# Feed-forward outputs of the first block: the upper four feature blocks of two weight tiles stand ahead of the wait for the SwiGLU products

## The reference

```python
def swiglu(h, w_in, w_out):
    a, g = jnp.split(h @ w_in, 2, axis=-1)
    return (jax.nn.silu(a) * g) @ w_out

    # in first_block, layer i
    x_lat = x_lat + mod_l[5] * swiglu(modulate(x_lat, mod_l[3], mod_l[4]), ffn_w_in[i], ffn_w_out[i])
    if need_ctx:
        x_ctx = x_ctx + mod_c[5] * swiglu(modulate(x_ctx, mod_c[3], mod_c[4]), ffn_w_in[i], ffn_w_out[i])
```

## Time and profile before

| | |
|---|---|
| median of 3 runs | 3102.27 us |
| lowest, highest | 3101.55, 3102.42 us |
| span of the profiled execution | 3102.3 us |
| TensorE busy | 2967.6 us, 96% |
| VectorE busy | 1898.2 us, 61% |
| ScalarE busy | 1184.0 us, 38% |
| mean rate of the DMAs | 153 GB/s |

### The profile page before, as it was taken

One profiled execution on the slowest core, in us unless ns is written; L12 is line 12 of the kernel. 1 busy time (PEld: TensorE's weight loads), 2 busy tenths in 40 slices (PEclk: granted clock), 3 DMA queues, 4 the chain that ended last, 5 costly groups with the idle time before them and its releaser, 6 DMA issues.

```text
span 3102.3 us, 49288 instructions
## 1 busy us (share of the span) xinstructions
PE 2967.6 (96%) x20168; PEld 2652.2 (85%) x20168; DVE 1898.2 (61%) x2575; ACT 1184.0 (38%) x1300; POOL 23.4 (1%) x33
## 2 busy tenths in 40 slices
PE   8999999999989899899999898999999999999998
PEld 5896887887867689899889887998899898888996
DVE  5754666675566655455557667654555476676554
ACT  5212223221154454333343534443433344425444
POOL 0000000000000000010000000000000000000000
PEclk9999999999999999999999999999999999999999
DMA  7420343444421145454544324555445543234454
GB/s 284 170 101 16 140 158 127 166 169 149 163 87 65 45 151 189 163 189 177 202 172 178 112 83 150 182 184 190 179 177 189 203 163 136 97 136 161 178 190 149
DMA packets 72066, 474.42 MB, mean 153 GB/s; under 512 B 8017, under 2 KB 9201, under 8 KB 20337
## 3 DMA queue, kind: packets, MB, share of 16 engines
q1 hardware_dynamic: 58352, 418.47, 37.1%
q10 hardware_dynamic: 11520, 41.95, 4.1%
q0 software_dynamic: 2048, 11.92, 1.0%
HBM read 471.26 MB, written 1.05 MB: 152 GB/s over the span
## 4 chain that ended last, share of the span: by engine, by line
PE 86%; DVE 7%; ACT 3%; DVEq 2%; issue 1%; DMA 0%; ACTq 0%; SPq 0%
PE ps L405 21%; PE ps L406 20%; PE ps L407 20%; PE ps L411 6%; PE ps L413 5%; PE ps L412 5%; DVE w_lo L1730 2%; PE ps L682 1%; ACT w_hi L1233 1%; DVE w_lo L1784 1%; PE ps L649 1%; PE ps L769 1%; PE ps L788 0%; PE ps L1125 0%; DMA raw<-in_ws 0%
## 5 line engine op out<-in xcount | busy, mean ns | idle before, releaser
L1730 DVE TENSOR_TENSOR w_lo<-raw,w_hi 128x2048 fp32r<-128x2048 f32 x371 | 850.6, 2293 | 685.8 <-ACT w_hi L1233 684.6
L1233 ACT CAST w_hi<-raw 128x2048 fp32r<-128x2048 f32 x369 | 702.3, 1903 | 1267.2 <-PE ps L407 910.4
L405 PE MATMUL ps<-l_hi,w_hi 128*128 128x256 f32 x2896 | 833.7, 288 | 16.2 <-DVE l_lo L1871 4.6
L406 PE MATMUL ps<-l_lo,w_hi 128*128 128x256 f32 x2896 | 824.0, 285 | 0.0
L407 PE MATMUL ps<-l_hi,w_lo 128*128 128x256 f32 x2896 | 823.7, 284 | 0.0
L405 PEld LDWEIGHTS ps<-l_hi,w_hi 128*128 128x128 f32 x2896 | 560.5, 194 | 28.0 <-issue 19.9
L406 PEld LDWEIGHTS ps<-l_lo,w_hi 128*128 128x128 f32 x2896 | 560.8, 194 | 0.3
L407 PEld LDWEIGHTS ps<-l_hi,w_lo 128*128 128x128 f32 x2896 | 560.4, 193 | 0.0
L405 PE MATMUL ps<-h_hi,w_hi 128*128 128x512 f32 (+1 forms) x1088 | 388.1, 357 | 20.1 <-DVE h_lo L1791 15.5
L406 PE MATMUL ps<-h_lo,w_hi 128*128 128x512 f32 (+1 forms) x1088 | 382.9, 352 | 0.0
L407 PE MATMUL ps<-h_hi,w_lo 128*128 128x512 f32 (+1 forms) x1088 | 382.8, 352 | 0.0
(11 more groups left out here) (453 smaller groups left out, 4003.1 us busy)
## 6 DMA issues: line engine op xcount, KB each, us to landing
raw<-in_ws SPq DMA_DIRECT2D x396, 1024.0 KB, 4.8
aT<-in_aw ACTq DMA_DIRECT2D x80, 512.0 KB, 3.6
ln_rows<-in_lnrow POOLq DMA_DIRECT2D x4, 1024.0 KB, 6.1
X<-in_xt SPq DMA_DIRECT2D x1, 2048.0 KB, 17.2
dist<-in_ret_dist POOLq DMA_DIRECT2D x1, 2048.0 KB, 14.0
relB<-in_relb POOLq DMA_DIRECT2D x2, 768.0 KB, 5.8
c_rows<-in_crow POOLq DMA_DIRECT2D x1, 1024.0 KB, 8.4
out<-X SPq DMA_DIRECT2D x1, 1024.0 KB, 4.8
```

The lines of the kernel that those rows point to most:

```text
L405: mm(out_, w_hi[:, s % SPLIT, blk], rhs_hi, start=start, stop=False)
L406: mm(out_, w_hi[:, s % SPLIT, blk], rhs_lo, start=False, stop=False)
L1233: nc.scalar.copy(w_hi[:, s % SPLIT], raw[:, raw_slot(s)]).then_inc(hi_done, 1)
L1730: tt(w_lo[:, raw_slot(s)], raw[:, raw_slot(s)], w_hi[:, s % SPLIT].bitcast(F32), ALU.subtract).then_inc(lo_done, 1)
```

## The change

TensorE's `ffn_out` takes the number of the `operand_ready` it needs as an argument, and waits for it later. It first waits for all groups but the last two, and multiplies tile 0 and then tile 1 for the upper four output blocks alone (m = 4 to 7, banks 4 to 7). Then it waits for all groups and multiplies both tiles for the lower four (banks 0 to 3), and raises `tile_used` for each behind its lower half. Only then does it wait for `operand_ready`, and tiles 2 to 9 follow in two turns of four. Tile 10 is as before. Tiles 0 and 1 read hidden blocks 0 to 3. No matmul is added or removed, and the other engines' programs are the same. The change is in both feed-forward parts.

```diff
-            def ffn_out(phase, cols, number, after=None):
+            def ffn_out(phase, cols, ready, after=None):
 
                 width = cols.stop - cols.start
+                s0 = PH[phase][0]
+
+                def part(t, blocks):
+                    for ci in range(2):
+                        for m in blocks:
+                            ins = product(ps[:, m, 0:width], ci * DC + m, s0 + t, hid_hi[:, 2 * t + ci, cols],
+                                          hid_lo[:, 2 * t + ci, cols], t == 0 and ci == 0, False)
+                    return ins
+                pe.wait_ge(sums_taken, group(phase, 0, 0))
+                for t in range(2):
+                    wait_tile(s0 + t, 0)
+                    part(t, range(4, DC))
                 pe.wait_ge(sums_taken, group(phase, 0, 2))
-
-                def body(first):
-                    def run(i, u, s, turn):
-                        wait_tile(s, turn)
-                        for ci in range(2):
-                            blk = bass.ds(i * 8 + 2 * (u + first) + ci, 1)
-                            for m in range(DC):
-                                ins = product(ps[:, m, 0:width], ci * DC + m, s, hid_hi[:, blk, cols], hid_lo[:, blk, cols],
-                                              first == 0 and ci == 0, False)
-                        ins.then_inc(tile_used, 1)
-                    return run
+                for t in range(2):
+                    part(t, range(4)).then_inc(tile_used, 1)
+                pe.wait_ge(operand_ready, ready)
+
+                def body(i, u, s, turn):
+                    wait_tile(s, turn)
+                    for ci in range(2):
+                        blk = bass.ds(i * 8 + 2 * (u + 2) + ci, 1)
+                        for m in range(DC):
+                            ins = product(ps[:, m, 0:width], ci * DC + m, s, hid_hi[:, blk, cols], hid_lo[:, blk, cols],
+                                          False, False)
+                    ins.then_inc(tile_used, 1)
...
-                tiles(phase, 0, pe, body(0), 0, 1)
-                tiles(phase, 0, pe, body(1), 1, 8)
-                tiles(phase, 0, pe, body(9), 9, 1)
+                tiles(phase, 0, pe, body, 2, 8)
                 tiles(phase, 0, pe, last, 10, 1)
...
-            pe.wait_ge(operand_ready, 4)
-            ffn_out("ffn_out0", slice(0, TT), 0, lambda c: squares(2, slice(0, TT), [c], SQ, 0))
+            ffn_out("ffn_out0", slice(0, TT), 4, lambda c: squares(2, slice(0, TT), [c], SQ, 0))
...
-            pe.wait_ge(operand_ready, 8)
-            ffn_out("ffn_out1", slice(0, T), 1)
+            ffn_out("ffn_out1", slice(0, T), 8)
```

## The result

| | before | changed |
|---|---|---|
| median | 3102.27 us | 3089.53 us |
| lowest, highest of 5 runs each | 3101.55, 3103.85 us | 3089.37, 3090.45 us |
| span of the profiled execution | 3102.3 us | 3087.3 us |

The ratio is 0.9957, with a 95% interval of 0.9946 to 0.9968: 12.7 us faster, by the interval between 9.9 and 16.8 us. The forecast was 3088.0 us in a range of 3086.0 to 3092.0 us.

What follows compares the result with a forecast made beforehand. TensorE was taken to bound the kernel (86% of the chain), losing time in idle and cold start ahead of both ffn_out phases. Gains of 10.27 and 3.97 us made 14.2 us: 3088.0 us, in a range of 3086.0 to 3092.0.

Steps and rivals of the forecast that it cites:

- The clock as a second price: At both ffn_out waits: besides the idle, TensorE restarts at 1.2 GHz, costing 2.45 us in ffn_out0 or 1.53 in ffn_out1.
- ffn_out0, 10.27 us: First feed-forward: tile 1 ends at 755.29 instead of 765.56; 7.8 us of idle and 2.45 of cold start go.
- margin at tile 2: ffn_out0: half a tile of matmuls, 5.44 us, covers tile 2's preparation of about 4.6 us, leaving 0.8 us, no stall.
- releaser of tile 3's high part: ffn_out0: tile 3's high part begins only behind the aT loads, which wait for VectorE to free buffers, at T0 + 9.87.
- ffn_out1, 3.97 us: Second feed-forward: tile 2 ends at 1263.03 instead of 1267.00, despite two new idles of about 1.5 us each.
- No clock lost behind the new idles: ffn_out1: nothing was taken for clock loss behind the two short idles; a cold start each, 1.53 us, was the upper bound.
- Rows 10 and 12: Profile rows of before: idles of 2.23 and 2.37 us behind full work, followed by stretches at clock 1.00.
- The sum, 14.2 us: Whole kernel: 10.27 us from ffn_out0 plus 3.97 us from ffn_out1, giving 3088.0 us.
- Nothing needs scaling: Whole kernel: the profiled span of 3102.3 us was taken as equal to the median of the runs, 3102.27 us.
- The clock in ffn_out1: Rival: the clock swings back behind the short idles, one or two cold starts, 1.5 to 3.1 us; chance 0.12.
- a broken margin: Rival: tile 1's or 2's margin in ffn_out0 fails, or later phases lose the gain, some 1 to 3 us; chance 0.10.
- The ring of aT loads: Rival: ffn_out0's chain of weight parts, ada halves and aT loads, 9.6 us a tile, eats the gain from 13.0; chance 0.03.

Runs made afterwards that it cites:

- run that kept the clock: Kernel before with 32 extra matmuls of 512 columns in the wait ahead of ffn_out0, their result overwritten: 3101.96 us against 3103.39.
- Six blocks ahead: Changed kernel, but in ffn_out0 six output blocks instead of four stand ahead for each of tiles 0 and 1: 3093.47 us.
- last bank late: Changed kernel, but in ffn_out1 tile 0 for seven output blocks, tile 1 for block 7, tile 0's last block, then tile 1's rest: 3087.11 us.
- form with one tile: Changed kernel, but in ffn_out1 only tile 0 is split, and tile 1 follows whole: 3090.37 us.
- ffn_out0 alone: Changed kernel with the old order put back in ffn_out1, so the new order stands in ffn_out0 only: 3093.72 us.
- 16 matmuls: Changed kernel with 16 extra matmuls of 512 columns between ffn_in0 and ffn_out0, their result overwritten: 3092.78 us.

## Why the prediction was right, point by point

- **The clock as a second price.** Right in kind; 2.45 us at ffn_out0 was the longest of four values (1.5 to 2.45), so the term is some 0.6 us above their mean of 1.8. The sizes come from stretches; the run that kept the clock couldn't show the price in the time. Taking it from one profiled execution was the weak step.
- **ffn_out0, 10.27 us.** Measured in the trace: 10.27. The margin at tile 2 was 0.88 us (0.8 said), the releaser of tile 3's high part changed to the aT buffers as said, 9.7 us behind the high part of tile 2 (759.26 - 749.54; about 9.6 said). Six blocks ahead showed the same cover from its other side.
- **ffn_out1, 3.97 us.** Measured: 3.86, with idles of 1.50 and 1.63 us (about 1.5 said, both on the low part of a tile). The run with the last bank late shows that short covers are their whole cause: too little of tile 0 ahead of tile 1 for the first, tile 0 held too long for the second.
- **No clock lost behind the new idles.** Right here, at 1.00 behind both, but with luck, for the reasons given don't carry. Rows 10 and 12 were read as idles of 2.23 and 2.37 us that full work makes harmless. At the place of the first of them the changed kernel has an idle of 2.25 us (first product at 1863.11), with the same matmuls and a clock of 1.00 in the 10.7 us ahead of it, and the clock behind it was 0.58 for 2 us. That the work between the two new idles protects the second was not tested. That it was close is shown as well by the form with one tile, where 2.69 us of idle cost 1.4 us. The Trainium skill ("TensorE: Matmul & The Clock Gate", "Why this matters for your kernels") warns only of gaps longer than that one; the trace differs, and the measurement decides.
- **The sum, 14.2 us.** The medians moved by 12.7, inside the interval of the ratio, and the spans of the two profiles by 15.0. Of these 15.0, 14.13 lie at the two sites (10.27 + 3.86); the rest is what other stages gained and lost: 2.1 us less elsewhere in the first block and 1.2 us more in the second. That the site stretches come out to 0.1 us says that the mechanism is right; it says nothing of the size of the cold start, since the stretch of before is the one the forecast was read from. Of the 1.5 us between 14.2 and 12.7 the cold start would explain 0.6; the rest is below what these runs can tell. "Nothing needs scaling" was wrong as a reading, since 1.7 to 2.2 us lie around a span and the profiled execution was a long one, but the sum was taken from the median and didn't lean on it.
- **Rivals.** The clock in ffn_out1 and a broken margin didn't come. The ring of aT loads is no bound at 9.7 us a tile (759.26 - 749.54), and becomes one at 12.3, with waits of the predicted length; its threshold for turning the whole gain was not tried.

## What to carry to other kernels

When work is pulled ahead of a wait by splitting tiles, it holds the tiles' buffers: compare what is left behind the release with the time in which the next tile is prepared (here 5.44 us against 4.6, fine, and 2.88 against 4.5, an idle of 1.6 us). Compare also what stands ahead of the second tile with the time since its own buffer came free. Hold back only the part that truly depends on the late result, here one bank of eight, and release the buffer early. And count a wait on TensorE as idle plus cold start, from several profiles rather than one.

## What the runs showed of the hardware

How long an idle is does not alone decide whether TensorE's clock falls. In the changed kernel, in the w_out stage of the second block, it fell behind an idle of 1.99 us with 3.8 us of full work ahead of it:

```profile
1883.80 0.67 PE L411 MATMUL ps<-w_hi,m_hi 128*128 128x512 f32 x1 [1.99 <-DVE w_lo L1739]
```

```profile
1878.00:1881.80 3.80, 3.80 (x17) 1.00 0.58 239
1883.80:1887.20 3.40, 3.40 (x8) 0.51 0.65 270
```

At the same place in the kernel before it stayed, behind an idle of 2.37 us:

```profile
1894.00:1898.00 4.00, 4.00 (x20) 1.00 0.58 246
1900.70:1904.00 3.30, 3.28 (x15) 1.00 0.58 243
```

Some 20 us earlier stands an idle that is the same in all 14 profiles, 2.23 to 2.25 us with the same instructions around it, ended by `mrt`. In 7 of them (the kernel before twice, the wait kept warm, ffn_out0 alone, six blocks, one tile, 16 matmuls) the clock was 1.00 in the 6 us behind it, and in the other 7, the changed kernel among them, it fell to the lower level:

```profile
1863.11 0.36 PE L405 MATMUL ps<-o_hi,w_hi 128*128 128x256 f32 x1 [2.25 <-DVE mrt L2609]
```

Idles of 1.50 and 1.63 us (ffn_out1) cost no clock in the changed kernel, and one of 2.69 us did in the form with one tile. So for one of about 2 us I would give no sign in advance. Such a stage then differs by some 1.6 us between profiles (20.7 against 19.1 us above); whether a shift upstream decides it, or the single execution, is not shown.
